# One kernel change: an output product with the attention's output held still and the weights streamed

## The reference, cut to what matters

```python
shift, scale, gate = jnp.split(jax.nn.silu(c) @ ada_w[i] + ada_b[i], 3, axis=-1)
h_lat = rms_norm_2(x, pre_norm[i]) * (1 + scale[:, None]) + shift[:, None]
shift_c, scale_c, gate_c = jnp.split(jax.nn.silu(c_ctx) @ ada_w[i] + ada_b[i], 3, axis=-1)
h_ctx = rms_norm_2(ctx, pre_norm[i]) * (1 + scale_c) + shift_c
...
y_lat = (o_lat * jax.nn.silu(g_l)) @ w_out          # (256 x 2048) @ (2048 x 2048)
x = x + gate[:, None] * rms_norm_2(y_lat, post_norm[i])
```

## Time and profile before

| | us |
|---|---|
| median of 3 runs | 1955.09 |
| lowest, highest | 1950.55, 1958.8 |
| the profiled execution | 1950.72 |
| its span, first to last instruction | 1948.9 |

### The profile page before, as it was taken

How to read it: one execution, slowest core, us unless ns; L and a number is a source line. 1 busy time by engine, 2 the same in 40 slices (tenths; PEclk the granted TensorE clock), 3 DMA queues, 4 the chain that set the end, 5 groups by cost and what they waited for, 6 DMA issues and landing times.

```text
span 1948.9 us, 27051 instructions
## 1 busy us (share of the span) xinstructions
PE 1802.2 (92%) x10641; PEld 1547.9 (79%) x10641; DVE 1416.7 (73%) x2242; ACT 817.5 (42%) x1294; POOL 7.2 (0%) x18
## 2 busy tenths in 40 slices
PE   6999988997888888999999999997989999999897
PEld 6899988987777777877777777775978966667697
DVE  5788758778899677887688768777772677777443
ACT  6544365624435444233332223224453444444353
POOL 1000000000000000000000000000000000000000
PEclk9999999999899989999999999998999999999999
DMA  6577744535566344345455536553442453434243
GB/s 213 191 260 260 229 154 152 184 97 171 193 227 227 109 150 126 113 141 173 135 197 183 191 129 204 185 192 107 130 138 76 145 170 110 136 109 150 78 152 98
DMA packets 169000, 311.11 MB, mean 160 GB/s; under 512 B 14908, under 2 KB 23464, under 8 KB 168872
## 3 DMA queue, kind: packets, MB, share of 16 engines
q1 hardware_dynamic: 162176, 305.70, 48.0%
q10 hardware_dynamic: 6248, 3.62, 0.7%
q0 software_dynamic: 448, 0.06, 0.0%
HBM read 307.23 MB, written 2.10 MB: 159 GB/s over the span
## 4 chain that ended last, share of the span: by engine, by line
PE 52%; DVE 7%; ACT 3%; issue 1%; DMA 0%; DVEq 0%; ACTq 0%
PE bank L503 15%; PE bank L504 15%; PE bank L505 15%; DVE w_low L316 2%; PE bank L2627 2%; PE bank L2626 1%; DVE ada_acc L431 1%; PE bank L2646 1%; PE bank L449 1%; ACT w_high L306 1%; PE bank L2637 1%; DVE big L682 1%; DVE big L2470 0%; DVE big L2469 0%; DVE operand L677 0%
## 5 line engine op out<-in xcount | busy, mean ns | idle before, releaser
L503 PE MATMUL bank<-operand,w_high 128*128 128x256 f32 (+1 forms) x2704 | 872.4, 323 | 73.1 <-DVE w_low L316 43.5
L504 PE MATMUL bank<-operand,w_high 128*128 128x256 f32 (+1 forms) x2704 | 860.2, 318 | 0.0
L505 PE MATMUL bank<-operand,w_low 128*128 128x256 f32 (+1 forms) x2704 | 860.1, 318 | 0.0
L503 PEld LDWEIGHTS bank<-operand,w_high 128*128 128x128 f32 x2704 | 529.5, 196 | 130.7 <-DVE w_low L316 50.2
L316 DVE TENSOR_TENSOR w_low<-raw,w_high 128x1024 fp32r<-128x1024 f32 (+4 forms) x416 | 454.1, 1127 | 187.9 <-ACT w_high L306 186.4
L306 ACT ACTIVATE w_high<-raw 128x1024 fp32r<-128x1024 f32 (+4 forms) x416 | 394.5, 980 | 426.7 <-PE bank L505 216.7
L504 PEld LDWEIGHTS bank<-operand,w_high 128*128 128x128 f32 x2704 | 529.5, 196 | 30.2
L505 PEld LDWEIGHTS bank<-operand,w_low 128*128 128x128 f32 x2704 | 528.9, 196 | 30.5
L431 DVE SCALAR_TENSOR_TENSOR ada_acc<-ada_raw,silu_c,ada_acc 128x512 f32<-128x512 f32 x720 | 489.2, 745 | 7.0 <-DMA ada_raw<-in_ada_w 4.7
L503 PE MATMUL bank<-operand_small,w_high 128*128 128x512 f32 (+1 forms) x320 | 123.6, 386 | 5.4 <-DVE big L414 3.3
L504 PE MATMUL bank<-operand_small,w_high 128*128 128x512 f32 (+1 forms) x320 | 119.7, 374 | 0.0
(11 more groups left out here) (372 smaller groups left out, 1384.3 us busy)
## 6 DMA issues: line engine op xcount, KB each, us to landing
ada_raw<-in_ada_w SPq DMA_DIRECT2D x192, 512.0 KB, 4.0
raw<-in_w_in SPq DMA_DIRECT2D x96, 512.0 KB, 5.0
raw<-in_pool_w_in SPq DMA_DIRECT2D x64, 512.0 KB, 5.2
raw<-in_mla_w_in SPq DMA_DIRECT2D x48, 512.0 KB, 4.5
raw<-in_w_out SPq DMA_DIRECT2D x32, 512.0 KB, 5.7
raw<-in_pool_w_out SPq DMA_DIRECT2D x32, 512.0 KB, 5.9
raw<-in_mla_w_out SPq DMA_DIRECT2D x32, 512.0 KB, 4.2
raw<-in_xa_wkv SPq DMA_DIRECT2D x16, 512.0 KB, 4.7
```

The source lines that it names most:

```text
L503: pe.matmul(out_, hi, x[:, 0, :], start=first, stop=False, skip_group_check=True)
L504: pe.matmul(out_, hi, x[:, 1, :], start=False, stop=False, skip_group_check=True)
L505: return pe.matmul(out_, lo, x[:, 0, :], start=False, stop=last, skip_group_check=True)
```

## The change

The output product is turned round. For each chunk, PE now holds 128 tokens of x still and streams the chunk's 512 weight columns: 2 halves of the tokens x 4 x 3 = 24 matmuls of 512 columns. Results have tokens on partitions. Banks alternate between 0, 1 and 2, 3 by group. ACT squares each result with a sum along the row (`SQS`), DVE multiplies it by the gate into `YT`, and at the end DVE adds four sums for each half of the tokens.

The gate must therefore be the same row on all partitions: the last four sums of the modulation are taken with a matmul by ones, DVE adds a bias and multiplies a gain that eight new DMAs from POOL bring to all partitions, and these rows are kept in the unused half of `XS`. For the last 32 units only the vector `c` is computed.

```diff
-                bank = n if p.banks == 4 else RINGS[p.banks][turn % len(RINGS[p.banks])]
+                bank = 2 * (i % 2) + n if p.kind == "token" else n if p.banks == 4 else RINGS[p.banks][turn % len(RINGS[p.banks])]
...
-    mo = Product("mo", mw_out, 4, 4, 4, 1, "gain1", dest=32, banks=4)
+    mo = Product("mo", mw_out, 4, 4, 2, 1, "token", width=GW, banks=4)
...
+            sides = 2 if u < 160 else 1
             for k in range(2):
-                for v in range(2):
+                for v in range(sides):
...
-                        dve.wait_ge(ada_link, 4 * u + 2 * k + v - 1)
+                        dve.wait_ge(ada_link, links(u) + sides * k + v + 1 - sides)
...
+            if b >= 20:
+                ins = pe.matmul(PB[3][:, :], ones[:, :], ACC[:, 0, :], start=True, stop=True)
...
+        def pool_gate_rows(pool):
+            pool.wait_ge(chunk_done, 2 * (mg23.chunk0 + mg23.chunks * mg23.groups))
+            for q in range(4):
+                bias = a["ada_b_2"][1:2, 2 * D + GW * q:2 * D + GW * (q + 1)]
+                gain = a["post_norm_2"][1:2, GW * q:GW * (q + 1)]
+                pool.dma_start(GATE_BIAS[q], halves(bias).to_broadcast([P, 2, T])).then_inc(gate_rows_in, 16)
+                pool.dma_start(GATE_GAIN[q], halves(gain).to_broadcast([P, 2, T])).then_inc(gate_rows_in, 16)
+
+        def dve_last_gates(dve, q):
+            dve.wait_ge(ada_summed, 21 + q)
+            if q == 0:
+                dve.wait_ge(gate_rows_in, 16 * 8)
+            gate_dve.inc(nc.vector.tensor_tensor(GATE[q], halves(PB[3][:, :]), GATE_BIAS[q], ALU.add), "b", q)
+            gate_dve.inc(nc.vector.tensor_tensor(GATE[q], GATE[q], GATE_GAIN[q], ALU.mult), "g", q)
...
+        def pe_tokens(pe, i, j):
...
+                for k in (2 * h, 2 * h + 1):
+                    x = XS[:, KC * j + k, :, n * P:(n + 1) * P]
+                    pe.matmul(bank, x[:, 0, :], HI[:, slot, k, :], start=j == 0 and k == 0, stop=False, skip_group_check=True)
+                    pe.matmul(bank, x[:, 0, :], LO[:, slot, k, :], start=False, stop=False, skip_group_check=True)
+                    ins = pe.matmul(bank, x[:, 1, :], HI[:, slot, k, :], start=False, stop=j == 3 and k == 3,
+                                    skip_group_check=True)
...
+        def act_squares(act, i, h):
+            wait_tile(act, mo, i, h)
+            end_act.inc(nc.scalar.activation(UNUSED, PB[mo.bank[i, h]][:, :], ACT.Square, accum_out=SQS[:, h, i:i + 1]), "q", i, h)
...
+        def dve_by_gates(dve, i, h):
+            end_act.wait(dve, "q", i, h)
+            cols = slice(GW * i, GW * (i + 1))
+            nc.vector.tensor_tensor(halves(YT[:, h, cols]), halves(PB[mo.bank[i, h]][:, :]), GATE[i], ALU.mult).then_inc(dve_freed, 1)
...
         def dve_mo(dve):
...
+            for h in range(2):
+                end_act.wait(dve, "q", 3, h)
+                end_dve.inc(v.tensor_reduce(RT[:, h:h + 1], SQS[:, h, :], AX.X, ALU.add), "s", h)
+                dve_by_gates(dve, 3, h)
+                end_act.wait(dve, "r", h)
+                end_dve.inc(v.reciprocal(RT[:, h:h + 1], RT[:, h:h + 1]), "r", h)
+                dve.wait_ge(dve_freed, mo.free0 + 7 + h)
+                for i in range(4):
+                    cols = slice(GW * i, GW * (i + 1))
+                    xt_act.wait(dve, "c", 2 * i + h)
+                    v.scalar_tensor_tensor(XT[:, h, cols], YT[:, h, cols], RT[:, h:h + 1], XT[:, h, cols],
+                                           ALU.mult, ALU.add).then_inc(out_ready, 1)
...
         def pe_mo(pe):
             la_act.wait(pe, "hi", 7)
             la_dve.wait(pe, "lo", 7)
-            for i in range(4):
...
-                    if c == 3:
-                        pe_rows(pe, 3)
...
-                    if i and j == 1:
-                        pe_turn_y(pe, i - 1)
...
-            for h in range(2):
-                ins = pe.matmul(PB[5][:, h:h + 1], ACC1[:, h * P:(h + 1) * P], ones[:, 0:1], start=True, stop=True,
...
+            for c in range(3, 16):
+                pe_tokens(pe, *divmod(c, 4))
+                if 4 <= c <= 11:
+                    pe_turn_x(pe, c - 4)
```

More of the change, by code:

```diff
@@ L2871, in build @@
         YT = BIG[:, 48:64, :].rearrange("p (a k) t -> p a (k t)", a=2)
-        ACC1, SQ1 = tile(68), [tile(64 + m) for m in range(4)]
+        piece = lambda n: (n // 2, n % 2, slice(GW * (n // 2), GW * (n // 2 + 1)))
+        UNUSED = wide(67)
+        SQS = small[:, 4:12].rearrange("p (i h) -> p h i", h=2)
         RT, SPARK = small[:, 0:2], small[:, 2:3]
-        piece = lambda n: (n // 2, n % 2, slice(512 * (n // 2), 512 * (n // 2 + 1)))
-        mo_dve = steps("mo_sums_dve", [("s", k) for k in range(1, 16)])
@@ new lines, in build, with part @@
+        end_dve = steps("end_dve", [(x, h) for h in range(2) for x in ("s", "r")])
+        def pe_tokens(pe, i, j):
+            c = mo.chunk0 + 4 * i + j
+            slot, end = c % 2, (i, j) == (3, 3)
+            def part(h, n):
+                if j == 0 and h == 0:
+                    pe_bank(pe, mo, i, n)
+                    if (i, n) == (1, 1):
+                        gate_dve.wait(pe, "b", 3)
+                bank = PB[mo.bank[i, n]][:, :]
+                for k in (2 * h, 2 * h + 1):
[4 more added lines that the diff above has]
+                                    skip_group_check=True)
+                return ins
+            if end:
+                for n in range(2):
+                    for h in range(2):
+                        pe.wait_ge(lo_ready, 2 * c + h + 1)
+                        ins = part(h, n)
+                    if n:
+                        ins.then_inc(chunk_done, 2)
+                    else:
+                        ins.then_inc(tile_done, 1)
+                return
+            for h in range(2):
+                pe.wait_ge(lo_ready, 2 * c + h + 1)
+                ins = part(h, 0)
+                if h == 1 and j == 3:
+                    ins.then_inc(tile_done, 1)
+                part(h, 1).then_inc(chunk_done, 1)
@@ L2909, in act_mo @@
                     if j == 0 and i:
-                        act_evac(act, mo, i - 1)
+                        for h in range(2):
+                            act_squares(act, i - 1, h)
                     if 6 <= c <= 13:
@@ L2914, in act_mo @@
                         xt_act.inc(s(XT[:, n % 2, piece(n)[2]], PB[4][:, :], ACT.Copy), "c", n)
[L2915 to L2918 removed]
             end_act.inc(s(SPARK, EPS, ACT.Sqrt), "spark")
[L2920 to L2922 removed]
+            for h in range(2):
+                act_squares(act, 3, h)
+                end_dve.wait(act, "s", h)
+                end_act.inc(s(RT[:, h:h + 1], RT[:, h:h + 1], ACT.Sqrt, bias=EPS, scale=1.0 / D), "r", h)
+        def dve_by_gates(dve, i, h):
+            end_act.wait(dve, "q", i, h)
+            cols = slice(GW * i, GW * (i + 1))
+            nc.vector.tensor_tensor(halves(YT[:, h, cols]), halves(PB[mo.bank[i, h]][:, :]), GATE[i], ALU.mult).then_inc(dve_freed, 1)
         def dve_mo(dve):
             v = nc.vector
[L2927 to L2929 removed]
             for i in range(4):
@@ L2933, in dve_mo @@
                         dve_low(dve, mo, i, j)
-                    if (i, j) == (0, 3):
-                        dve_gates(dve, 1, 3)
-                    if i and 4 * (i - 1) + j:
-                        add(4 * (i - 1) + j)
-            for k in range(12, 16):
-                add(k)
-            end_act.wait(dve, "r")
-            end_dve.inc(v.reciprocal(RT, RT), "r")
-            for n in range(8):
-                _, h, cols = piece(n)
-                if n < 6:
-                    yt_act.wait(dve, "c", n)
-                else:
-                    yt_pe.wait(dve, "t", n)
-                xt_act.wait(dve, "c", n)
-                y = YT[:, h, cols] if n < 6 else PB[6 + h][:, :]
-                v.scalar_tensor_tensor(XT[:, h, cols], y, RT[:, h:h + 1], XT[:, h, cols], ALU.mult, ALU.add).then_inc(out_ready, 1)
+                    if j == 0 and i:
+                        for h in range(2):
+                            dve_by_gates(dve, i - 1, h)
+            for h in range(2):
+                end_act.wait(dve, "q", 3, h)
[9 more added lines that the diff above has]
+                                           ALU.mult, ALU.add).then_inc(out_ready, 1)
         def pe_mo(pe):
```

95 lines of the change are left out of this document (24 added, 71 removed).

## The result

| us | before | after |
|---|---|---|
| median of 6 runs each | 1951.26 | 1929.64 |
| lowest, highest | 1947.02, 1958.80 | 1927.52, 1934.22 |
| profiled execution | 1950.72 | 1928.11 |
| its span | 1948.9 | 1926.3 |

The ratio is 0.9889, with a 95% interval of 0.9874 to 0.9903: 1.1% faster, 21.6 us by the medians and 22.6 us by the spans. Of these 7.4, 3.8 us are the level: with more runs the median of before fell from the 1955.1 on which the forecast stood to 1951.3. The other 3.5 us or so are gain that the sum had too small.

A forecast was written before the change was run, and what follows sets the result against it. PE's instruction stream was taken to set the pace. Gains of 3.7 + 1.3 + 0.9 + 4.2 + 3.6 + 2.6 - 0.3 + 2.3 = 18.3 us from 1950.7 gave 1932.4, or 1936.8 against the 1955.1 median; range 1930 to 1946.

The forecast's parts named there:

- Term 1: Last four modulation sums: one vector instead of two drops a matmul of 0.93 us four times, gaining 3.7 us.
- term 2: Halved DVE work in the 32 last units: closes seven waits before the last probabilities, +1.3, and the first rope wait, +0.9.
- Term 3: Output product: 384 matmuls of 512 columns at 0.229 us instead of 768 of 256, gaining 4.2 us.
- Term 4: Output product: chunk 4 no longer waits, 2.1 us, and the clock's fall behind the gap goes, 1.5 us; together +3.6.
- 5, turns of y: PE's stream: three `pe_turn_y` of 0.87 us each go, gaining 2.6 us.
- 6, behind chunks 7 and 11: PE's wait for a turned piece of x grows by 0.16 us, twice: -0.3 us.
- Term 7: From the product's last matmul to DVE's end: 6.3 us instead of 8.56, gaining 2.3 us.
- drain behind it: Output DMAs behind DVE's end: the same eight, their 3.9 us left unchanged, gain 0.
- Term 8: POOL's eight new DMAs: 0, hidden by 57 us of attention; delayed units bounded at -1.5 in place of +0.9.
- A: Sum holds but one term fails (`mo` clock, weight streaming or step 0's DMAs): gain 14 to 17, 1938 to 1941; chance 0.23.
- B: Weights' supply becomes the bound in `mo`: gain 8 us, 1947; chance 0.12, with any loss of that size.
- C: Gate's rows from POOL's DMAs come late and DVE waits: slower, 1965 to 1971; chance 0.05.

The follow-up runs named there:

- e2: Changed kernel with PE taking each of the last four sums twice into the same bank: 1931.32 us, ratio 0.9900 to the kernel before.
- e8: Changed kernel with the last four sums' ones 48 columns wide instead of 128: 1928.27 us, ratio 0.9874 to the kernel before.
- e1: Changed kernel with DVE again computing both vectors in the last 32 units, the second unused: 1936.68 us, ratio 0.9924 to the kernel before.
- e11: As e1, but POOL's eight DMAs wait until PE has done step 0's keys and values: 1933.13 us, ratio 0.9900 to the kernel before.
- e3: Changed kernel with each 512-column matmul of the output product cut into two of 256: 1933.25 us, ratio 0.9905 to the kernel before.
- b1: Kernel before with 12 filler matmuls in PE's idle gap between chunks 3 and 4: 1950.78 us, ratio 0.9988 to the kernel before.
- e9: Kernel before with its last eight multiply-adds and output DMAs ordered by token half: 1950.51 us, ratio 0.9987 to the kernel before.
- e4: Changed kernel with its last chunk in the order of the others, no token half finished early: 1931.42 us, ratio 0.9901 to the kernel before.
- e5: Changed kernel with a PE wait put back between chunks 3 and 4: 1930.26 us, ratio 0.9897 to the kernel before.
- e5b: Same edit of the changed kernel as e5, run again for a second profile: 1930.90 us, ratio 0.9899 to the kernel before.
- a0: The changed kernel once more, no edit: 1928.11 us, ratio 0.9887 to the kernel before.
- e6: Changed kernel with 34 unread filler matmuls in PE's four waits of steps 8 and 9: 1927.34 us, ratio 0.9883 to the kernel before.
- e7: As e6, plus 25 filler matmuls at the barrier before `pairs`: 1924.87 us, ratio 0.9874 to the kernel before.
- f_best: Changed kernel with the fillers of e6 and e7 and POOL's DMAs after step 0: 1924.72 us, ratio 0.9853 to the kernel before.

## Why the prediction was too careful

The sign, the order of size and the mechanisms that the forecast named were right. Two things were not: the level that the gain was taken from, and the sizes of four terms, all too small. No term was too large by more than 0.2 us. Measured, with chance parts taken out:

| term | forecast | measured | from |
|---|---|---|---|
| 1, one vector in the sums | 3.7 | 4.8 | steps with a sum; e2, e8 |
| 2, waits for probabilities | 1.3 | 2.8 | e1, e11, 0.40 x 7 |
| 2, first rope | 0.9 | 0.8 | 2.60 to 1.81, start to start |
| 3, wide matmuls | 4.2 | 4.4 | e3 |
| 4, chunk 4 | 3.6 | 3.7 | timelines (2.2), b1 (1.5) |
| 5, turns of y | 2.6 | 2.4 | 3 x 0.80 |
| 6, behind chunks 7 and 11 | -0.3 | -0.3 | 7.32 - 5.84 and 7.21 - 5.56 |
| 7, tail | 2.3 | 3.1 | 8.56 - 5.46 |
| drain behind it | 0 | 1.0 | 3.93 - 2.9; e9 |
| sum | 18.3 | 22.7 | |

From 22.7 a longer half-speed stretch before chunk 3 took back about 1.5, and the start of `pairs` gave 1.2 by chance: 22.4, against 22.6 in the spans. That these two nearly cancel is luck.

**The steps that failed.** The largest single one is the step from the sum to a time, "so against the median I predict 1936.8": 3.8 of the 7.4 us. It took the median of three runs as the level, and six runs have it at 1951.26. In the sum itself it is term 2, "it closes the wait before the last probabilities ... seven times, +1.3", which measured 2.8. It took the idle time that the trace shows, 0.18 each. That idle time is counted from the modelled end of the matmul before, and the count from start to start, which terms 1, 3 and 4 used, was not applied here. The kernel before, at the first of the seven:

```profile
1609.26 1.05 PE L2646 MATMUL bank<-big 128*128 128x128 f32 x8
1610.49 0.66 PE L2637 MATMUL bank<-ident,big 128*128 128x128 f32 x4 [0.18 <-DVE big L2789]
...
1611.11 0.28 PE L504 MATMUL bank<-operand,w_high 128*128 128x256 f32 x1
```

From the first line to the last is 1.85 us, and 1608.74 - 1607.29 = 1.45 in the kernel after: 0.34 in front of the transposes and 0.06 behind them, 0.40 each, 2.8 in all. This is the largest of the mis-sized terms; the next three are as follows.

**Term 1** priced the matmul left out well (0.87 against 0.93). It overlooked that the remaining one has another shape, 128 columns held still instead of 48, and that was worth another 0.33 a sum (e8).

**Term 7** built the second half as "reciprocal to multiply-add 0.5". That 0.49 in the earlier trace rows held a wait of 0.32; after, it is 1917.07 - 1916.88 = 0.19, once for each half, so 0.6 us. The remaining 0.2 is the multiply by the gate: 0.70 was its duration, and from start to start it is 1920.52 - 1919.91 = 0.61, twice. The early first half gave 1.36 (e4), as the forecast had it.

**The drain**, "I leave their 3.9 us", was not left: the new code writes one token half after the other, and the old kernel with that order alone has 3.16 (e9). The order of the DMAs had changed in the diff, and the prediction looked at their number only.

**Term 3** held, at 0.2268 a matmul with the weights streaming as with x streaming. Halving them again cost 0.25 to 0.30 us a chunk, 24 x 0.0104 to 24 x 0.0125. The gap formula of the Trainium skill ("TensorE: Matmul & The Clock Gate", "Back-to-back issue gap"), which that section gives for an isolated matmul and not for a stream, would have made that, as an estimate, 24 x 2.5 ns = 0.06 us a chunk and 1.0 us in all; the runs show more than four times as much, and they decide.

**Term 4** held in size, with one half of its reason. The fall of the clock behind the old gap was real and the gap's (b1). "If some other gap makes the clock fall as well" was the right thing to fear: a 1.56 us gap at the same place did not (e5, e5b), but the waits of the last pair did, in each of the thirteen profiles without fillers there. These stretches varied: 3.4 us (before, e8, e5b), twice 3.4 (e1, e3), 10.2 (after, a0, e2, e4, e5, e9, e11, b1), in both kernels. What chooses between them was not found; that PE's idleness there brings them was (e6, e7, f_best: none).

**Term 8** came to 0 by two effects that the prediction had apart. It had bounded at -1.5 that POOL's bytes delay the units, and said of DVE's halved work that it closes the first rope wait. Both are so, and in the profile after the second paid for the first: part of the 40 us of freed DVE time, "nearly all of it worth nothing", was the cover without which those DMAs cost 7.5 us in step 1 in one execution (39.60 in e1 against 32.12 in e11). The cover is thin. In four of the ten profiles with one vector and the early DMAs (e3, e4, e5b, e8) PE does wait for the first rope, 0.69, 0.22, 0.68 and 1.04 us, so term 2's +0.9 is not there in every execution.

**The rivals.** A fell as a forecast of the time, since its terms held; its clock clause came true in another place, where the longer half-speed stretch reached into chunk 3 and took 1.5 us. B fell: in `mo` PE waited for weights nowhere; only once before it, 0.2 us at chunk 1. C was half seen: POOL does pause, for 7.64 and 5.66 us, but after three DMAs, not after each, so all were issued by 1579 where C needed 85 us. The box on DVE and GpSimd's DMAs in the Trainium skill ("SBUF — State Buffer") would have made the issue longer while DVE is in a two-port mode. The issue took 0.72 to 0.77 us against 0.53 for 24 rows, and no row names DVE's mode, so the runs do not test that rule. It cannot be the whole of the pause of 7.64 us, from 1560.84 to 1568.49: DVE had no work from 1565.53 to 1569.31. What POOL waits for is open.

**The level.** The span was turned into a median by "that execution lies 4.4 us under the median of 1955.1". Three runs had a median 3.8 us too high; against all six the profiled execution lies 0.5 us under it. On the level of six runs the same sum of 18.3 gives 1933.0. The low end was also drawn short of its own words: 1936.8 less 0.9, 0.5 and 4 is 1931.4, not 1930.

## What to carry to other kernels

Take the price of a short wait on PE from start to start, as that of a matmul: 0.18 us of idle time shown was 0.40 us of stream. When an instruction is kept but changes shape, or a set of DMAs is kept but changes order, it is still a part of the change with a price. Work taken off an engine that is not the bound may be what hides another part of the same change, so test the two together before calling either free; and an idle gap of PE is worth filling where the trace shows half speed behind it, which gave 3.2 us in the profiled stage here.

## What the runs showed that was not expected

- POOL issued three DMAs of 256 KB to 128 partitions at 0.77, 0.74 and 0.73 us, then paused 7.64 us, issued three more, paused 5.66 us and issued two, with nothing in the profile that it waited for. The thirteen traces with these DMAs all have three, three and two, with pauses of 4.1 to 8.0 us. They landed 5.7 and 6.5 us after issue (medians), and meanwhile a unit's weights from SP came late enough to hold DVE for 3.17 us.
- A sum of fp32 matmuls of 512 columns, set between the products, cost 0.33 us more of PE's stream with 48 columns held still than with 128: once a sum, not once a matmul.
- The clock's stretch at 1.2 GHz behind the same waits of the same kernel was 3.4, 6.8 or 10.2 us long from one execution to another. At the barrier before `pairs` there was one of 3.4 us in eleven of the fourteen profiles without fillers there; the stage was 1.5 us shorter in the three others, which have 6.8 us at half speed some 16 us earlier.
- Eight output DMAs of 256 KB, last issued by token half instead of by column block, ended 0.8 us sooner behind DVE's last instruction.
